# Three of four MLP down products with tokens on partitions, summed there and added by identity matmuls

## What is computed

```python
def sqrelu_mlp(hn, w_up, w_down):          # w_up 2048 x 8192, w_down 8192 x 2048
    return jnp.square(jax.nn.relu(hn @ w_up)) @ w_down

h = h + sqrelu_mlp(rms_norm(h, norm_mlp[l]), w_up[l], w_down[l])
```

## Time and profile before

| | |
|---|---|
| median of 3 runs | 2578.92 us |
| the profiled execution | 2576.89 us |
| its span | 2575.2 us |
| PE busy | 2414.0 us (94%), 18299 matmul records |
| PEld busy | 2319.8 us (90%) |
| POOL busy | 2060.9 us (80%) |
| ACT busy | 1044.5 us (41%) |
| DVE busy | 953.4 us (37%) |
| the MLP in the span | about 900 to 1640 us |
| L598, matmuls of 128x256 with `hidden` | 3072 records |

### The profile page before, as it was taken

One profiled execution on the slowest core, in us unless ns is written; L12 is line 12 of the kernel. 1 busy time (PEld: TensorE's weight loads), 2 busy tenths in 40 slices (PEclk: granted clock), 3 DMA queues, 4 the chain that ended last, 5 costly groups with the idle time before them and its releaser, 6 DMA issues. The chain is left out here.

```text
span 2575.2 us, 45181 instructions
## 1 busy us (share of the span) xinstructions
PE 2414.0 (94%) x18299; PEld 2319.8 (90%) x18299; DVE 953.4 (37%) x1451; ACT 1044.5 (41%) x1308; POOL 2060.9 (80%) x1940
## 2 busy tenths in 40 slices
PE   6999999988998899999999999999799998999896
PEld 6989998768997799999999999999799888988896
DVE  6025662554152442031021130704516662255422
ACT  3344444554345333333333333434334333344532
POOL 6988894766786599899899999798797986865583
PEclk9999998999998899999999999999899998999998
DMA  5654433353443355555555555465354554533241
GB/s 176 194 172 144 148 121 120 115 196 115 164 147 115 115 178 182 184 177 195 182 179 181 180 184 195 148 196 163 119 178 149 165 187 147 163 114 114 100 164 50
DMA packets 206437, 400.31 MB, mean 155 GB/s; under 512 B 10434, under 2 KB 20932, under 8 KB 205252
## 3 DMA queue, kind: packets, MB, share of 16 engines
q1 hardware_dynamic: 206276, 397.99, 47.5%
HBM read 395.87 MB, written 2.10 MB: 155 GB/s over the span
## 5 line engine op out<-in xcount | busy, mean ns | idle before, releaser
L565 POOL TENSOR_TENSOR w_low<-ring,w_high 128x512 fp32r<-128x512 f32 (+3 forms) x1872 | 2051.2, 1128 | 470.1 <-ACT w_high L1070 465.4
L1070 ACT ACTIVATE w_high<-ring 128x1024 fp32r<-128x1024 f32 (+2 forms) x760 | 786.5, 1039 | 1373.2 <-PE bank L598 1357.5
L598 PE MATMUL bank<-x_high,w_high 128*128 128x256 f32 x4196 | 1219.8, 291 | 80.6 <-issue 32.8
L598 PE MATMUL bank<-x_low,w_high 128*128 128x256 f32 x4196 | 1203.7, 287 | 0.0
L598 PE MATMUL bank<-x_high,w_low 128*128 128x256 f32 x4196 | 1203.2, 287 | 0.0
L598 PEld LDWEIGHTS bank<-x_high,w_high 128*128 128x128 f32 x4196 | 822.5, 196 | 96.7 <-issue 51.5
L598 PEld LDWEIGHTS bank<-x_low,w_high 128*128 128x128 f32 x4196 | 822.8, 196 | 2.0 <-issue 1.8
L598 PEld LDWEIGHTS bank<-x_high,w_low 128*128 128x128 f32 x4196 | 822.0, 196 | 0.0
L598 PE MATMUL bank<-hidden,w_high 128*128 128x256 f32 x2048 | 368.8, 283 | 0.0
L598 PEld LDWEIGHTS bank<-hidden,w_high 128*128 128x128 f32 x2048 | 319.5, 192 | 0.0
L598 PE MATMUL bank<-hidden,w_low 128*128 128x256 f32 x1024 | 289.8, 283 | 0.0
(11 more groups left out here) (265 smaller groups left out, 1721.1 us busy)
## 6 DMA issues: line engine op xcount, KB each, us to landing
ring<-in_w_in SPq DMA_DIRECT2D x64, 1024.0 KB, 5.4
ring<-in_w_up SPq DMA_DIRECT2D x64, 1024.0 KB, 5.2
ring<-in_w_down SPq DMA_DIRECT2D x64, 1024.0 KB, 5.0
ring<-in_w_out SPq DMA_DIRECT2D x48, 1024.0 KB, 5.0
ring<-in_a_w_in SPq DMA_DIRECT2D x32, 1024.0 KB, 5.3
ring<-in_b_w_in SPq DMA_DIRECT2D x32, 1024.0 KB, 5.3
ring<-in_w_kv SPq DMA_DIRECT2D x24, 1024.0 KB, 5.2
ring<-in_w_mem_kv SPq DMA_DIRECT2D x16, 1024.0 KB, 5.0
```

The source lines that it names most:

```text
L565: last = pool.tensor_tensor(w_low[:, u % UNITS, part], ring[:, u // 2, first:first + n], w_high[:, u % UNITS, part], ALU.subtract)
L598: mm = pe.matmul(out, lhs, rhs, start=start and n == 0, stop=stop and n == 2, skip_group_check=True)
L1070: act.activation(w_high[:, u % UNITS, 0:n], ring[:, u // 2, r0 * g.width:r0 * g.width + n], ACT.Copy)\
```

## The change

Down products 0 to 2 use the tokens form. VectorE copies down0's blocks into `down_rows` (tiles 32 to 47 of `proj`, fp32, tokens on partitions) and adds down1's and down2's to it, in place of the additions into `hT`. Down3 keeps the features form, with its loop written out by hand; after unit 0 of each of its blocks 8 matmuls, with `down_rows` as weights and the 128x128 identity `ident` moving, transpose the sum of the three and add it into the block's banks.

```diff
+        down_rows = proj[:, 32:48, :].rearrange("p a t -> p (a t)").rearrange("p (h n) -> p h n", h=TH)
...
+            def add_down_rows(j, pair):
+
+                for f in range(4):
+                    for h in range(TH):
+                        col = (f % 2) * T + h * P
+                        pe.matmul(pair[f // 2][:, col:col + P], down_rows[:, h, (4 * j + f) * P:(4 * j + f) * P + P],
+                                  ident[:, :], start=False, stop=False, skip_group_check=True)
+
             for part in range(4):
                 product(f"up{part}", features_unit, operand, made=x_made["mlp"] if part == 0 else None, sums=norm_sum)
-                product(f"down{part}", features_unit, hidden_tile, made=4 * part + 1, ready=hidden_ready)
+                if part < 3:
+                    product(f"down{part}", tokens_unit, hidden_tile, made=4 * part + 1, ready=hidden_ready)
+
+
+            g = PLAN["down3"]
+            for j in range(4):
+                group_free(g.g0 + j)
+                for u in range(8):
+                    if j == 0 and u % 2 == 0:
+                        pe.wait_ge(hidden_ready, 13 + u // 2 + 1)
+                    if u == 1:
+                        add_down_rows(j, pair_of(g.g0 + j))
+                    features_unit(g, g.b0 + j, u, pair_of(g.g0 + j), hidden_tile, 4 * (u // 2), KT)
...
+            def added_rows(v):
+                return lambda n, c, b: dve.tensor_tensor(v[:, c, bass.ds(n * 512, 512)], b[:, :],
+                                                         v[:, c, bass.ds(n * 512, 512)], ALU.add)
+
...
-                if part < 3:
-                    residual(f"down{part}")
+                if part == 0:
+                    keep("down0", rows(down_rows))
+                elif part < 3:
+                    dve.wait_ge(evacuated, PLAN[f"down{part}"].g0)
+                    keep(f"down{part}", added_rows(down_rows))
             residual_and_operand("down3", 0, G_2A)
```

## The result

The changed kernel takes **2564.3 us** (median of 5 runs, 2563.62 to 2565.42) against 2578.92 for the kernel before (5 runs): ratio 0.9941, 95% interval 0.9929 to 0.9953, or 14.6 us less. The forecast of the sign was right; 8.2 us were forecast, and the time lies 1.7 us under the range. Measured twice more, on other occasions, it gave 0.9937 and 0.9951.

What follows compares the result with a forecast made beforehand. PE was taken to set the pace in the MLP, with GpSimd's slack only 0.33 us a unit. Terms -15.4 and +7.2 us, the others 0, gave -8.2 us: 2570.7 us from a median of 2578.92, range 2566 to 2577.5.

Steps and rivals of the forecast that it cites:

- Part 1: Down0 to down2 in the tokens form: 0.16 us gained in each of 96 units, -15.4 us.
- Rival B: Tokens units of down0 to down2: overhead isn't in the weight load, gain only 2.9 us, time 2583.2 us; chance 0.02.
- Part 2: GpSimd in down0 to down2: falls 2.2 us behind in each first block, unseen by PE; 0, or 6.6 us uncovered.
- A: GpSimd's subtractions in down0 to down2 become the bound, 2.86 us a unit, time 2584.2 us; chance 0.04.
- C: Half the gain lost, to PE's GpSimd waits in first down blocks or 0.43 us identity matmuls: 2577.3 us; chance 0.10.
- part 6: SP's DMAs, ScalarE and the stage after the MLP: same order, the stall moves along unchanged, 0.
- Part 3: VectorE's read-out of the down blocks: two operations per block stay two, 0.
- 5: Down3 written out instead of a loop: instruction fetch nearly the same, bound -3 to +3 us, taken as 0.
- Part 4: 32 identity matmuls in down3, 0.224 us each with nothing hiding them: +7.2 us.
- Rival D: Identity matmuls in down3 cost one record each, 3.6 us in all, time 2567.1 us; chance 0.05.
- the signs: Profile expected if right: down0 to down2 read-outs 21.76 us apart, MLP 8 us shorter, all else unchanged.

Runs made afterwards that it cites:

- r3: The changed kernel without the 32 identity matmuls: 2564.83 us, ratio 0.9943 to the kernel before.
- r4: The changed kernel with down0 to down2 back in the features form, identity matmuls and down_rows additions kept: 2586.00 us, ratio 1.0025 to the kernel before.
- r5: The changed kernel with 43 dummy fp32 matmuls ahead of down3's first identity matmuls: 2579.45 us, ratio 0.9995 to the kernel before.
- r14: Repeat of the changed kernel with 43 dummy fp32 matmuls ahead of down3's first identity matmuls: 2578.81 us, ratio 1.0000 to the kernel before.
- r13: Repeat of the changed kernel with only down0 in the tokens form, down1 and down2 added to hT: 2574.84 us, ratio 0.9985 to the kernel before.
- r16: The changed kernel without edit, measured a third time: 2565.23 us, ratio 0.9951 to the kernel before.

## Why the prediction was right and wrong

**Part 1, the tokens form: right.** -15.4 us was forecast, three times 5.10 = -15.3 measured. The 13 ns per matmul and weight load hold: a unit takes 2.72 us in the down products as it did in hgrn_v. The 2.5 ns of the Trainium skill ("TensorE: Matmul & The Clock Gate", "Back-to-back issue gap"), which that section gives for a single, isolated matmul, would have made it 2.9. Rival B is out.

**Part 2, GpSimd: right.** It fell behind where said and made it good unseen, with 0.34 us of idle per two units then, not 0.24. Rivals A and C are out. That VectorE and GpSimd slow each other was seen here (1.43 us a subtraction) but only as a price for GpSimd. It has one for VectorE too: its squaring ahead of down0 took 6.45 us, where the like step of the earlier trace rows took 2.19. In the MLP this hides; in part 6 it doesn't.

**Part 3 and 5: right**, nothing showed in the MLP.

**Part 4, the identity matmuls: the price right, the cover wrong.** One costs 24.75 - 22.97 = 1.78 us by eight, 0.223 each, as L803 said. But "nothing hides them" fails in the last block: VectorE sets the end there, and 0.35 of 1.8 us is exposed: 5.7 us in all instead of 7.2. Rival D, one record each, is out. I had read that PE sets the pace in the MLP as a whole; the last 8 us belong to VectorE, and its timeline would have shown it.

**Part 6 failed, and it put the time outside the range.** It said of the stage after that the "stall moves along unchanged", and the signs said "all else unchanged": the 1850 us outside the MLP got the term 0. Pool_in itself did move along. Behind it the stages are not the same length when they start elsewhere. By the medians this was 4 to 5 us, half as much again as the net effect of the change by its parts: 8.2 becomes 9.6 with the cover, and 14.6 with this. The range was made from the terms of the MLP alone; 9.6 us would have lain in it. That the remainder fell on the side of a gain is luck: r3 and r4 changed the MLP just as exactly and got none of it.

What the traces show in its place: PE's wait for VectorE ahead of out0 (8.9 us where GpSimd holds up VectorE's cast, 4.8 where it doesn't) and dense work that falls into half-clock stretches. Together they make the stretch to out0 252.9 us in the changed kernel and 254.8 in before's second trace and in r5 and r14, 1.9 us less. Behind out0's first read-out two of the changed kernel's three traces have 676.2 us where those three have 678.3, and the third has 679.6. That is 4 us in two traces; the rest is open, with before's median moving by up to 4. The first trace of before was itself one with a short cast (251.1), so the pair of profiles in the result's table doesn't show this gain.

This too is why the removal of the identity matmuls gains nothing: its traces have the long cast, 256.2 us to out0 instead of 252.9, and 678.6 instead of 676.2 us behind, 5.7 us in all.

The cause of the 4 to 5 us is known as far as this: not in the MLP (traces), not in the new code as such (r4, r5, r14), repeated by kernel (r13 to r16), and seen in the traces as the two terms above. No run tested the cast by itself, and why this kernel falls well and its neighbours by 1 us don't is not explained.

## What to carry over

Where a product is bound by matmuls that each load their weights, the form with 512 moving columns saves the fixed part of every second matmul (13 ns here), at the price of a transposition that can be shared by summing products first. Ask of each added step who sets the end in that very block. And where later stages have VectorE and GpSimd at work side by side with PE waiting, or idle time and half-clock stretches, give a small gain a margin of several microseconds: a term that is exact to 0.01 us in its own stage can grow by half or vanish behind it. To see which, compare PE's idle time first and its clock second.

## What was not expected of the hardware

- One VectorE cast of 128x1024 took 0.69 us with GpSimd idle, 1.15 us in one trace beside it and 6.23 in another, and PE's wait behind it 4.8 or 8.9 us. In the two traces of the unchanged kernel it was once short and once long.
- Work in a dense stage repeats to 0.01 us from trace to trace (MLP 714.22, 714.22, 714.21), while the same instructions in stages with idle gaps spread over 7 us.
- Taking 5.7 us of TensorE work away from the MLP left the total where it was, twice (2564.83 and 2564.86 beside 2566.07 and 2565.23); 0.7 us of added work cost 3.9 (0.5 to 6.7).
- A plain fp32 matmul of 128 columns with new weights costs 0.223 us in two records, as long as 512 columns in fp32r (0.227 us).
